# GLU inputs, convolution and LayerNorm of a hybrid encoder step, split between the first two token tiles and the later three

## The reference

```
h = rmsnorm(x, norm1_g) * (1 + sc1) + sh1            # sh1.. from silu(c) @ w_ada (2048 x 12288)
za, zg, q, k, v = split(h @ w_in)                     # five parts of 1024 columns
u = za * sigmoid(zg)
y_conv = causal_dwconv(concat(conv_left, u), w_dw, b_dw)   # 31 taps, each channel for itself
y_conv = silu(layernorm(y_conv, conv_ln_g, conv_ln_b))
o = banded attention of 16 heads x 64, with clipped relative bias
x = x + g1 * (concat(y_conv, o) @ w_out)
h2 = rmsnorm(x, norm2_g) * (1 + sc2) + sh2
x = x + g2 * peer(h2)
```

## Time and profile before

| | us |
|---|---|
| median of 3 runs (4137.07 to 4159.22) | 4140.31 |
| the profiled execution's own time | 4138.69 |
| its span in the profile | 4136.9 |
| PE busy | 3599.0 (87%) |
| DVE busy | 2778.2 (67%) |
| POOL busy | 1119.9 (27%) |
| ACT busy | 445.1 (11%) |
| DMA moved | 1401.81 MB, mean 339 GB/s |

### The profile page before, as it was taken

The page is one execution under the profiler, slowest core; times in us unless marked ns, Lnnn a source line. Parts: engine busy times, 40 slices in busy tenths (PEclk is TensorE's granted clock), DMA queues, the critical chain, the costliest instruction groups (busy, mean ns, idle before and its releaser), DMA issues.

```text
span 4136.9 us, 33604 instructions
## 1 busy us (share of the span) xinstructions
PE 3599.0 (87%) x11871; PEld 1898.6 (46%) x11871; DVE 2778.2 (67%) x5020; ACT 445.1 (11%) x1077; POOL 1119.9 (27%) x858
## 2 busy tenths in 40 slices
PE   3699998987997789788689999999868999996992
PEld 0366644456553564355633444444353444442440
DVE  2128872227878996779976666776797676654677
ACT  1100002210000230011800000000080000000000
POOL 1100000005545443345043223222404322221233
PEclk7799998998999679899899999999989999998996
DMA  9978753349999999899199999999919999999997
GB/s 351 231 235 259 247 186 126 125 146 389 402 401 411 370 351 356 344 367 377 76 408 420 421 416 412 421 419 420 392 67 390 418 418 421 420 422 392 421 410 295
DMA packets 356524, 1401.81 MB, mean 339 GB/s; under 512 B 22353, under 2 KB 146457, under 8 KB 219110
## 3 DMA queue, kind: packets, MB, share of 16 engines
q0 software_dynamic: 116720, 831.77, 50.6%
q1 hardware_dynamic: 239072, 563.91, 36.5%
q10 hardware_dynamic: 576, 4.19, 0.2%
HBM read 1369.87 MB, written 31.42 MB: 339 GB/s over the span
## 4 chain that ended last, share of the span: by engine, by line
DMA 46%; PE 26%; issue 12%; DVE 11%; POOL 3%; ACT 1%; another core or an unknown queue 0%; SPq 0%; DVEq 0%; POOLq 0%; ACTq 0%
DMA R<-in_u_experts,MS 32%; PE bank L805 10%; DMA R<-in_v_experts,MS 8%; PE bank L781 8%; PE bank L985 3%; POOL R L677 3%; DVE R L1808 3%; DMA R<-in_w_ada 2%; DVE R L2014 2%; DVE R L1898 2%; PE bank L735 1%; DMA R<-in_w_pq 1%; DMA R<-in_w_out 1%; DVE R L1807 1%; PE bank L712 1%
## 5 line engine op out<-in xcount | busy, mean ns | idle before, releaser
L677 POOL DMA_INDIRECT R<-in_u_experts,MS x640 | 915.0, 1430 | 1776.2 <-DVE MS L1898 1532.2
L1898 DVE CUSTOM_DVE_ANT_0 R<-R 128x2048 f32<-128x2048 f32 x368 | 844.6, 2295 | 418.7 <-DMA R<-in_u_experts,MS 395.6
L1151 PE MATMUL bank<-R,RB 128*128 128x512 f32 x2304 | 1018.3, 599 | 78.9 <-DMA R<-in_v_experts 78.8
L1151 PE MATMUL bank<-RB 128*128 128x512 f32 x1792 | 778.2, 592 | 0.0
L1151 PEld LDWEIGHTS bank<-R,RB 128*128 128x128 f32 x2304 | 439.4, 192 | 647.7 <-issue 547.8
L1898 DVE CUSTOM_DVE_ANT_0 R<-R,RB 128x2048 f32<-128x2048 f32 x272 | 622.1, 2287 | 123.3 <-DMA R<-in_u_experts,MS 122.3
L805 PE MATMUL bank<-R,RB 128*128 128x512 f32 x1216 | 531.8, 599 | 21.2 <-DMA R<-in_w_in 12.4
L1151 PEld LDWEIGHTS bank<-RB 128*128 128x128 f32 x1792 | 340.5, 190 | 428.6 <-issue 428.6
L781 PE MATMUL bank<-RB,R 128*128 128x256 f32 (+1 forms) x1536 | 403.2, 424 | 28.7 <-DMA R<-in_w_pq 22.4
L2014 DVE SCALAR_TENSOR_TENSOR R<-R,MS 128x2048 f32<-128x2048 f32 x128 | 301.4, 2355 | 186.2 <-DMA R<-in_v_experts,MS 185.1
L805 PEld LDWEIGHTS bank<-R,RB 128*128 128x128 f32 x1216 | 232.8, 192 | 314.9 <-issue 290.6
(11 more groups left out here) (296 smaller groups left out, 2010.4 us busy)
## 6 DMA issues: line engine op xcount, KB each, us to landing
R<-in_v_experts SPq DMA_DIRECT2D x144, 1024.0 KB
RB<-in_v_experts SPq DMA_DIRECT2D x112, 1024.0 KB
R<-in_w_ada SPq DMA_DIRECT2D x48, 2048.0 KB, 13.0
R<-in_w_in SPq DMA_DIRECT2D x32, 2048.0 KB, 18.5
R<-in_w_out SPq DMA_DIRECT2D x16, 2048.0 KB, 11.6
R<-in_w_pq SPq DMA_DIRECT2D x16, 2048.0 KB, 21.8
R<-in_u_experts,MS POOLq DMA_INDIRECT x640
RB<-in_x_prompt POOLq DMA_DIRECT2D x6, 1024.0 KB, 15.3
```

The costliest lines, as they stand in the source:

```text
L677: pool.indirect_dma_start(dst, None, table, bass.IndirectOffsetOnAxis(ap=expert[T_ % 2][:, c:c + 1], axis=0)).then_inc(signal, 16)
L1151: x = pe.matmul(PB[4 * h + q][:, :], W[:, i, h * P:(h + 1) * P], vring[slot][:, q * PW:(q + 1) * PW], start=(i == 0), stop=(i == NKEY - 1))
L1898: V.tensor_tensor_reduce(u, u, x, 1.0, 0.0, ALU.mult, ALU.add, dots[t % 2][:, h * TOPK + s:h * TOPK + s + 1]).then_inc(dots_done, 1)
```

## The change

It deals with the GLU inputs, the convolution and its LayerNorm.

- The GLU stage projects `hTX` alone (256 columns instead of 640), and `conv`, the channel sums and LayerNorm there have 256 columns. A tap is one instruction that waits for the one before.
- Behind the key queries of X, TensorE projects za and zg of Y in four further blocks (16 groups of 384 columns), for which SP loads these 16.8 MB of w_in once more. The order there is za and zg in turn (4 blocks), k (2), v (2, with `rows_out` around them), q (2, a channel sum behind each).
- The cache of the samples is loaded behind `s_cat` on POOL, turned in front of these blocks, and copied by ScalarE.
- VectorE: `steps(124)` becomes `steps(50)`; then, for each half of the channels, four `gated_later` and 15 times 8 taps and one dot, and 4 taps; then 4 dots, the subtraction of the mean, 12 dots, the variance, 1 dot, and the products. The attention of Y follows.
- All `rows_out` now run in the later part. SP stores their rows (`later_rows`). The first values of Y have three buffers, reused once.

The diff, cut to its core:

```diff
+    FIRST, TAPS, MEAN, SQUARES = 50, 8, 4, 12
...
             sp.wait_ge(s_ext, 16)
-            sp.wait_ge(s_conv, 1)
-            sp.wait_ge(s_uc, 1)
             for h in range(4):
                 first_bias(h)
...
-            for n in range(12):
+            for n in range(20):
                 if n < 2:
                     sp.wait_ge(q_done, 14 + 2 * n)
...
+                block = n // 2
+                if block < 4:
+                    col = (block % 2) * CC + block // 2 * PW
+                else:
+                    col = (3, 4, 2)[block // 2 - 2] * CC + block % 2 * PW
+                load_half(n, "w_in", col, w_in_s)
+                if n == 13:
+                    later_rows(0)
+                    later_rows(1)
+                if n == 15:
+                    values_out(0)
+                    later_rows(2)
+                    later_rows(3)
+                if n == 17:
+                    values_out(1)
+                    later_rows(4)
+            sp.wait_ge(s_conv, 2)
+            k_cache(0)
...
                 if hp == 1:
                     pool.wait_ge(z_free, 2 + 28)
-                    for i in range(2, 4):
-                        rows_stored(i)
+                    for t in range(TX):
+                        dma(kvo["k", 0][t], ost[:, t]).then_inc(s_ost[t], 16)
+                    pool.wait_ge(s_cat, CT)
+                    ccv = ins["cache_conv"].rearrange("l (h b) k c -> (l h) (b k) c", h=2)
+                    for h in range(2):
+                        dma(ccx[:, h], ccv[h]).then_inc(s_cc, 16)
...
-                        project((hTX, hTY), ring[:, b, :, c * P:(c + 1) * P], c, z_done)
+                        project((hTX,), ring[:, b, :, c * P:(c + 1) * P], c, z_done)
...
-                    pe.matmul(PB[bank][:, 0:NP], mean_w, src(c)[:, 0:NP], start=(c == 0), stop=(c == CT - 1))
-                    m = pe.matmul(PB[bank + 1][:, 0:P], mean_w, src(c)[:, NP:NT], start=(c == 0), stop=(c == CT - 1))
+                    m = pe.matmul(PB[bank][:, 0:n], mean_w, src(c), start=(c == 0), stop=(c == CT - 1))
...
-                if h in (3, 6):
-                    rows_out(h // 3 - 1)
...
+            for b in range(6):
+                later_columns(28 + 4 * b, b == 0)
+            pe.wait_ge(z_free, 2 + 52)
+            pe.wait_ge(cc_E, 4)
+            rows_out(0)
+            rows_out(1)
+            later_values(0)
+            pe.wait_ge(s_u, 16)
+            rows_out(2)
+            pe.wait_ge(s_uc, 3)
+            rows_out(3)
+            later_values(1)
+            rows_out(4)
+            later_columns(58, True)
+            pe.wait_ge(s_oE, 5)
+            pe.wait_ge(s_conv, 2)
+            channel_sum(6, lambda c: conv_outY[:, c], NY, None, 0, None).then_inc(s_mean, 1)
+            later_columns(62, False)
+            channel_sum(7, lambda c: ysqY[:, c % 2], NY, s_ysq, CT, s_ysq_used)
...
+                    if j:
+                        act.wait_ge(s_vsty[t], 16)
+                    A(vstY[t], PB[v][:, :], ACT.Copy).then_inc(z_free, 1)
...
-            steps(124)
+            steps(FIRST)
+
+            def gated_later(c):
+                dve.wait_ge(z_free, 2 + 33 + 8 * (c // 4) + c % 4)
+                TT(uY[:, c, CTX:], uY[:, c, CTX:], sigY[:, c, 0:NPY], ALU.mult)
+                TT(uS[:, c, :, CTX:], uS[:, c, :, CTX:], sigY[:, c, NPY:NY].rearrange("p (b s) -> p b s", s=NS),
+                   ALU.mult).then_inc(s_u, 1)
...
+                        dve.wait_ge(s_dve, ch.base + at_tap[1] - 1)
+                        ch.mark(STT(out=oP, in0=iP, scalar=w, in1=oP, op0=ALU.mult, op1=ALU.add))
+                        dve.wait_ge(s_dve, ch.base + at_tap[1])
+                        ch.mark(STT(out=oS, in0=iS, scalar=w, in1=oS, op0=ALU.mult, op1=ALU.add))
+                    at_tap[0], at_tap[1] = at_tap[0] + 1, ch.n
+
+            for half in range(2):
+                for c in range(4 * half, 4 * half + 4):
+                    gated_later(c)
+                for i in range(4 * WID // TAPS):
+                    later_taps(TAPS)
+                    steps(1)
+                later_taps(4 * WID % TAPS)
+            ch.sync()
+            dve.sem_inc(s_conv, 1)
+            steps(MEAN)
+            dve.wait_ge(s_mean, 2)
+            for c in range(CT):
+                TT(conv_outY[:, c], conv_outY[:, c], PB[6][:, 0:NY], ALU.subtract).then_inc(s_xc, 1)
+            steps(SQUARES)
+            dve.wait_ge(s_ysq_used, 2 * CT)
+            v, r = ysqY[:, 0], ysqY[:, 1]
+            ch.link(TS(v, PB[7][:, 0:NY], EPS, None, ALU.add))
+            dve.sem_inc(s_lnv, 1)
+            steps(1)
+            dve.wait_ge(s_lnr, 2)
+            ch.link(V.reciprocal(r, r))
+            ch.link(refine(r, v, lntY))
+            for c in range(CT):
+                TT(conv_outY[:, c], conv_outY[:, c], r, ALU.mult).then_inc(s_lnx, 1)
```

More of the change, by code:

```diff
@@ L248, in hybrid_encoder_step @@
         s_osty = [sem(f"rows_stored_{i}") for i in range(2)]
-        s_vsty = [sem(f"later_v_stored_{i}") for i in range(2)]
+        s_vsty = [sem(f"later_v_stored_{i}") for i in range(TY)]
         s_cso = sem("conv_cache_moved")
@@ L460, in _ @@
+                if n == 17:
[3 more added lines that the diff above has]
+            k_cache(0)
+            for n in range(20, 22):
                 load_half(n, "w_out", 0, w_in_s)
-            values_out(1)
             def values(hp):
@@ L513, in _ @@
             x1_out(2, slice(0, 3 * PW))
-            for n in range(20, 22):
+            for n in range(28, 30):
                 load_half(n, "w_pq", 0, w_q)
@@ L521, in _ @@
                 sp.dma_start(h2_d[t], x1[t]).then_inc(s_h2s, 16)
-            for n in range(22, 28):
-                load_half(n, "w_pq", (n - 20) // 2 * PW, w_q)
+            for n in range(30, 36):
+                load_half(n, "w_pq", (n - 28) // 2 * PW, w_q)
             sp.wait_ge(q_done, 32)
@@ L987, in half_columns, with later_columns @@
                 return m
-            for b in range(4):
+            pe.wait_ge(s_cc, 32)
+            for c2 in range(4):
+                for i in range(4):
+                    c, h = 2 * c2 + i // 2, i % 2
+                    t = tr(PB[4 + c2][:, i * 120:(i + 1) * 120], ccx[:, h, c * P:(c + 1) * P], 120)
+                t.then_inc(cc_T, 1)
+            def later_columns(n0, first):
                 for half in range(2):
@@ L1000, in _, with later_values @@
                             m.then_inc(w_used, 1)
-            for i in range(4, 7):
-                pe.wait_ge(z_free, 2 + 44)
-                rows_out(i)
-            for j in range(2):
+            def later_values(j):
                 for half in range(2):
@@ L1086, in _ @@
             pe.wait_ge(pv_read, 2 * NH)
+            pe.wait_ge(s_cat, 2 * CT)
             for j in range(4):
@@ new lines, in _ @@
+            act.wait_ge(s_oE, 5)
+            for c in range(4):
+                keep_columns(58 + c, catY[:, CT + c], -DH ** -0.5, 2)
+            for i in range(TY):
+                act.wait_ge(s_vsty[i], 16 * 2)
+            for c in range(2):
+                later_squares(c)
+            for c in range(4, CT):
+                keep_columns(58 + c, catY[:, CT + c], -DH ** -0.5, 2)
+            for c in range(2, CT):
+                later_squares(c)
+            act.wait_ge(s_lnv, 2)
+            A(ysqY[:, 1], ysqY[:, 0], ACT.Sqrt).then_inc(s_lnr, 1)
@@ L1962, in _ @@
             dve.wait_ge(s_const, 3)
[L1963 to L1966 removed]
+            for i in range(2):
+                dve.wait_ge(s_ost[i], 16)
+            dve.wait_ge(s_vsty[2], 16 * 2)
             ch.link(V.memset(qX, 0.0))
```

293 lines of the change are left out of this document (137 added, 156 removed).

## The result

| | before | after |
|---|---|---|
| median of the runs, us | 4138.78 (4137.07 to 4159.22, 4 runs) | 4262.32 (4242.99 to 4271.79, 4 runs) |
| profiled execution, us (span) | 4138.69 (4136.9) | 4271.79 (4270.0) |

The ratio on record is 1.0273, with a 95% interval of 1.0242 to 1.0304 (the two medians alone give 1.0298): slower, by 123.5 us of medians and 133.1 us between the two profiled executions. The forecast was 4260.

The account below looks back on a forecast made before the run. TensorE was taken to bound 196 to 695 us, gathers by DMA 941 to 1370, VectorE 1370 to 1555, with `burst(0)` a fixed point. Terms -91 + 141 + 70 = +120 on 4138.69 gave 4260, own range 4205 to 4310.

Parts of the forecast that it names:

- part 1: GLU stage on the first tiles alone: steps of 16.3 instead of 21.0 us, bound by loads, 70 us earlier (30 to 90).
- part 2's 3 us for the cache: Ahead of the first dot: the cache's 983 KB leave a full DMA and 16 transposes leave TensorE, 3 us earlier.
- part 2: Rest ahead of the first dot: channel sums 10, SiLUs 5, two `rows_out` 3, cache 3 us earlier.
- part 3: First dot to second attention: TensorE's added columns bound it, 570 against 429 us, 141 us later (125 to 165).
- part 4: 27 dots put off past the second attention leave about 30 before `burst(0)`, with TensorE idle: +70 us (45 to 90).
- behind dot 272: After `burst(0)`, which stands in front of dot 272 and opens the dense pass over V: nothing added, no gather removed.
- (a): Rival: TensorE falls to its low clock in the GLU stage, steps 21 us, 4329 us; chance 0.11 with slower yet.
- (b): Rival: put-off dots are free, VectorE making good 27 in gaps of output projection or key queries, 4189 us; chance 0.12.
- (c): Rival: DMA bounds the way to dot 272, only the second reading of GLU weights counts, 4090 us; chance 0.08.
- (d): Rival: a convolution tap waits its full latency, 0.80; 33 us on VectorE behind TensorE's 551, sum unchanged; no chance given.

Follow-up runs that it names:

- a_same: The kernel after the change, run once more unaltered as the base for the other runs: 4254.99 us, ratio 1.0245 to the kernel before.
- b_joint: The kernel after, with the GLU stage projecting all 640 columns again, the later 384 unread and computed again later: 4340.69 us, ratio 1.0466.
- b_half_ada: The kernel after, without loading the second half of the rows of each w_ada block in the GLU stage: 4178.33 us, ratio 1.0081.
- d_before_few: The kernel before, with 14 of the 16 conv-row transposes left out of the first attention: 4156.45 us, ratio 1.0022.
- a_half_taps: The kernel after, without taps 15 to 30 of the later tokens' convolution, the number of dots kept: 4260.78 us, ratio 1.0248.
- b_short_glu: The kernel after, without seven of eight matmuls in the later tokens' four GLU column blocks: 4199.57 us, ratio 1.0124.
- c_before_97: The kernel before, with 97 instead of 124 dots ahead of the second attention: 4189.29 us, ratio 1.0102.
- a_fill: The kernel after, with 26 put-off dots put back ahead of the second attention, into VectorE's waits: 4205.02 us, ratio 1.0121.
- b_third: The kernel after, with the GLU stage projecting 384 instead of 256 tokens, the third tile's results unread: 4267.53 us, ratio 1.0282.
- a_clock: The kernel after, with eight unused identity transposes at each of two places in the first attention where `rows_out` stood: 4245.18 us, ratio 1.0209.

## Why the prediction was right, and where it was not

The forecast of 4260 stands 2 us from the median, but two of its terms were off in opposite directions, and the kernel's own median moved from 4262 to 4255 in a_same, so the closeness is partly luck. By steps:

| step | forecast | profile after | profile of a_same |
|---|---|---|---|
| part 1, GLU stage | -70 | -84 | -86 |
| ahead of the stage (part 2's 3 us for the cache) | -3 | -4 | -4 |
| part 2, stage to first dot | -18 | +4 | 0 |
| first dot, sum of these | -91 | -85 | -89 |
| part 3, first dot to second attention | +141 | +140 | +134 |
| part 4, from there to dot 272 | +70 | +75 | +65 |
| behind dot 272 | 0 | +3 | 0 |
| sum | +120 | +133 | +109 |

**Part 1** was right in its mechanism and too careful in its size. Fifteen steps took from 191.78 to 422.4 us, 15.4 each, where 16.3 was taken: almost the bare load time of 15.0. At a DMA share of 1.04 hardly any of the gap that was added for reissue and landing is left. b_joint and b_half_ada show both sides, the stage bound by TensorE at 21 us and by loads at 15.4, with TensorE's own work at 10.7.

**Part 2 is where the prediction failed**, in the term of 3 us for the two `rows_out` that leave the first attention. They were counted by their own duration alone. In fact the clock rose to 2.4 GHz at them, and without them the attention runs at 1.2: +9.8 us in place of -3, as d_before_few shows. The row that would have told it was in the trace of before: scores of 1.22 us ahead of the transposes and 0.70 behind. The channel sums and SiLUs came out as forecast (3.62 and 4.82 us for the sums, 4.04 us for eight SiLUs); stage to first scores shrank by 13.6 of the 15 us forecast. The last 7.4 us, from the last scores to the first dot, had no forecast, and the traces show slow stretches in them too: 2.3 us are the last weighings, 3.0 lie in the output projection, whose first 16 us have a granted clock of 0.81 where it was 1.00, and 2.1 in the first key queries (64 records in 16.17 us where they took 14.08). The size varies: the fourteen profiles have 183 to 191 us for this path, a_same 187. So the attention without its transposes cost 12 us in all, and what follows it up to 5 more.

**Part 3** held in its mechanism, and its match to 1 us is luck, since a_same has 562.8 for the same way: TensorE bound, 569.4 against 570, with the mean of the later tokens at 1352 and VectorE waiting 47.5 us for the mean where the forecast's own figures give 45 (551 less the last block of 41.8 and a sum of 5, against 448 and four dots of 2.75). a_half_taps shows that VectorE's path has slack, and b_short_glu that TensorE's is still last after 53 us have gone. The columns of the fourth gate came 197 us behind the first dot, where 195 was forecast. That late weights could be left out held as well, with 8.2 us of waits for w_in.

**Part 4** held as well: 29 dots ran between the last key scores and the burst where about 30 were forecast, in 95 us where 85 were. c_before_97 (79 us for 27 dots) and a_fill (56 us at `burst(0)` for 26 dots brought back) give it from two sides.

**The rivals.** (a), TensorE at the low clock in the GLU stage, would have had steps of 21 us; they are 15.4. Its mechanism was there all the same: of the 21 groups of 32 modulation records that waited for w_ada, 13 took 2.62 to 3.60 us where 1.91 is full speed, and the granted clock of the stage is 0.89. The Trainium skill, "TensorE: Matmul & The Clock Gate", part "HAM oscillation — how this bites in real kernels", has such a loop restart slowly behind every wait; the trace agrees in part, since the other 8 groups ran at full speed, one of them behind 3.95 us of idle time (234.84). The projection behind a slow group is slower too, up to 8.22 us instead of 7.17. But all this is at most some 4 us of a step which has 5 us to spare; b_third, whose projection is half as long again, waits only 8 times and has a clock of 0.96 in the stage. (b) falls by a_fill and c_before_97. (c), a way that the DMA engines bound, falls by their share of 0.78 and 0.70 there: what it would have needed, TensorE's blocks ahead of the loads, wasn't so. b_short_glu made it so for the four short blocks, and there the loads did bound TensorE. (d) makes no difference, by a_half_taps.

## What to carry to other kernels

Work that is moved doesn't cost at its new place what it took at the old one. Taking 15 times 10.2 us of TensorE's work out of the stage gave 84 us, because the loads became the bound; the same columns behind the first dot stood in front of a barrier for which TensorE was last, and there they counted in full. Count fillers by position, too: when a filler (a dot) is taken out of a wait to make room for other work, find where it falls next and who is idle there. And look at the rate of the matmuls around each piece that you take out, for a piece can be what brings the clock up. Last, when a cut of 146 us gives back 53, look for what the engine waits on now: here it was its own weights, and not the engine that was expected next.

## What the runs showed of the hardware

- A stretch of small matmuls with hardly a gap (TensorE busy for 56.99 of 58.00 us, 64 rows or 64 columns in most) stayed at the granted clock of 0.50 to its end, in each profiled execution that had no run of transposes in it (the kernel after and eight others).
- Where it fell: in the kernel before and the kernel after alike the rows are slow from the transposes that follow an idle time of TensorE of 3.96 and 3.99 us.
- What lifted it: eight transposes of the form 128*30 in the kernel before and in c_before_97, and 24 of the form 128*128 in two kernels. Eight of the latter did not in the profiled execution of a_clock. Why eight are enough in one kernel and not in the other isn't settled.
- The loads of the stage moved 336 GB/s with a DMA share of 1.04, their blocks in rows of 1 KB, where the stretch ahead of the second attention, three quarters of it gathers of rows of 8 KB, moved 402 at a share of 1.01 in the kernel before.
- The spread of one kernel goes with the mean granted clock. Of the eleven executions of the kernel before beside a_same the shortest (4134.57 us) had 0.934 and the longest (4173.94 us) 0.924; in c_before_97 4166.46 us had 0.932 and 4210.06 us 0.918. What moves the clock from one execution to the next is not shown.
